# A hybrid encoder block with 32 experts: 0.75 MB of a weight unit loaded by an earlier instruction, and two spread parts placed before the last down product instead of behind it

## The reference, cut to what matters

```python
x = x + jnp.concatenate([a, p], axis=-1) @ w_out[l]
h = rmsnorm(x, xattn_norm_g[l])
x = x + memory_cross_attention(h, rmsnorm(mem, mem_norm_g[l]), ...)   # softmax(q k / sqrt(128)) v @ xo_w
h = rmsnorm(x, ffn_norm_g[l])
x = x + hierarchical_moe(h, ...)
# per expert e, on the tokens routed to it:
(jax.nn.silu(xb @ w_gate[e]) * (xb @ w_up[e])) @ w_down[e]            # 2048 -> 512 -> 2048
```

## Time and profile before

| | us |
|---|---|
| three runs | 1671.82, 1673.2, 1670.22 (median 1671.82) |
| the profiled execution | 1668.66 |
| its span, first to last instruction | 1666.9 |
| PE busy | 1553.7 (93%) |
| DVE busy | 637.7 (38%) |
| ACT busy | 357.5 (21%) |
| data read and written | 484.81 MB and 8.39 MB (millions of bytes) |

### The profile page before, as it was taken

The page is one execution under the profiler, slowest core; times in us unless marked ns, Lnnn a source line. Parts: engine busy times, 40 slices in busy tenths (PEclk is TensorE's granted clock), DMA queues, the critical chain, the costliest instruction groups (busy, mean ns, idle before and its releaser), DMA issues.

```text
span 1666.9 us, 18187 instructions
## 1 busy us (share of the span) xinstructions
PE 1553.7 (93%) x7236; PEld 894.2 (54%) x7236; DVE 637.7 (38%) x774; ACT 357.5 (21%) x639; POOL 165.2 (10%) x235
## 2 busy tenths in 40 slices
PE   7999999999999999799999899889889899899998
PEld 7788777768887567634343433434434334343343
DVE  6656656652223433513233322322323323323224
ACT  6422333352222244211110110011011011101011
POOL 4470044510000000100000000000000000000000
PEclk9999999999999999999999999999999999999999
DMA  8332322353215031799999999999999999999997
GB/s 304 102 101 79 94 61 70 103 183 101 96 56 202 1 127 44 320 377 429 412 424 429 428 428 429 428 423 420 429 417 417 428 420 428 428 426 428 424 421 290
DMA packets 90237, 484.47 MB, mean 291 GB/s; under 512 B 6066, under 2 KB 44108, under 8 KB 62156
## 3 DMA queue, kind: packets, MB, share of 16 engines
q1 hardware_dynamic: 86696, 470.84, 69.8%
q0 software_dynamic: 3392, 12.92, 2.3%
q10 hardware_dynamic: 100, 0.03, 0.0%
HBM read 484.81 MB, written 8.39 MB: 296 GB/s over the span
## 4 chain that ended last, share of the span: by engine, by line
PE 68%; DMA 17%; DVE 8%; ACT 3%; issue 2%; SPq 1%; POOL 0%; DVEq 0%; POOLq 0%; ACTq 0%
PE ps L2232 23%; DMA weight_ring<-in_expert_w_up_dram 15%; PE ps L1939 10%; PE ps L1813 8%; PE ps L2258 8%; PE ps L2193 5%; PE ps L1992 3%; DVE residual L1618 3%; ACT weight_ring L887 1%; PE ps L1775 1%; DMA residual<-in_x_dram 1%; PE ps L2321 1%; PE ps L2056 1%; DVE weight_ring L1290 1%; PE ps L2081 1%
## 5 line engine op out<-in xcount | busy, mean ns | idle before, releaser
L2232 PE MATMUL ps<-weight_ring,transposed_acts 128*64 128x512 f32 x2000 | 467.6, 610 | 40.2 <-DMA weight_ring<-in_expert_w_up_dram 39.4
L2232 PEld LDWEIGHTS ps<-weight_ring,transposed_acts 128*64 128x64 f32 x2000 | 169.0, 140 | 331.6 <-issue 260.1
L1618 DVE TENSOR_TENSOR residual<-ps,residual 128x1024 f32<-128x1024 f32 x128 | 150.8, 1219 | 249.6 <-PE ps L2193 249.2
L2258 PE MATMUL ps<-weight_ring,transposed_acts 128*64 128x512 f32 x960 | 214.1, 599 | 17.8 <-DVE transposed_acts L1628 17.8
L1634 DVE SCALAR_TENSOR_TENSOR y_low<-ps,proj_buffer,y_high 64x1024 fp32r<-64x1024 f32 x60 | 77.0, 1283 | 199.4 <-ACT y_high L1079 198.4
L2258 PEld LDWEIGHTS ps<-weight_ring,transposed_acts 128*64 128x64 f32 x960 | 67.6, 138 | 146.8 <-issue 142.7
L1079 ACT ACTIVATE y_high<-ps,proj_buffer 64x1024 fp32r<-64x1024 f32 x60 | 66.5, 1109 | 288.1 <-PE ps L2258 287.3
L1813 PE MATMUL ps<-mix_high,w_in_high 128*128 128x512 f32 x288 | 117.8, 409 | 1.3 <-issue 1.3
L1068 ACT ACTIVATE transposed_acts<-ps 128x512 f32<-128x512 f32 x32 | 19.1, 598 | 464.7 <-PE ps L2232 464.7
L1813 PE MATMUL ps<-mix_high,w_in_low 128*128 128x512 f32 x288 | 112.8, 392 | 0.0
L1813 PE MATMUL ps<-normed_low,w_in_high 128*128 128x512 f32 x288 | 112.7, 391 | 0.0
(11 more groups left out here) (323 smaller groups left out, 1889.3 us busy)
## 6 DMA issues: line engine op xcount, KB each, us to landing
weight_ring<-in_expert_w_down_dram SPq DMA_DIRECT2D x63, 2048.0 KB, 15.8
weight_ring<-in_expert_w_gate_dram SPq DMA_DIRECT2D x61, 2048.0 KB, 16.3
weight_ring<-in_expert_w_up_dram SPq DMA_DIRECT2D x60, 2048.0 KB, 20.5
weight_ring<-in_w_in_dram SPq DMA_DIRECT2D x18, 1024.0 KB, 5.6
weight_ring<-in_w_out_dram SPq DMA_DIRECT2D x16, 1024.0 KB, 5.0
weight_ring<-in_xkv_w_dram SPq DMA_DIRECT2D x8, 1024.0 KB, 7.6
residual<-in_x_dram SPq DMA_DIRECT2D x8, 1024.0 KB, 12.8
weight_ring<-in_xq_w_dram SPq DMA_DIRECT2D x4, 1024.0 KB, 9.7
```

The source lines that it names most:

```text
L1618: v.tensor_tensor(part, ps[:, bank:bank + 2, :].rearrange("p b n -> p (b n)"), part, ALU.add).then_inc(signal, 1)
L2232: ins = mm(ps[side * SLOTS:(side + 1) * SLOTS, 0, :], xsT[:, k, par * SLOTS:(par + 1) * SLOTS], gate_up_weights(e, u, kk), start=(k == 0), ...
L2258: ins = mm(ps[half, 4 + n % 2, :], act_t[:, f * SLOTS:(f + 1) * SLOTS], w[:, n * 512:(n + 1) * 512], start=(f == 0), stop=(f == KF - 1), s ...
```

## The change

It has two parts.

1. Of expert 1's unit 3 the floats 2048 to 3583 of each partition (the first 1536 floats of slot 7, 0.75 MB) are loaded by an instruction of their own, issued once `oT_ready` has reached 4. What is left, slot 6 (1 MB) and the last 512 floats of slot 7 (0.25 MB), is loaded at the old place by two instructions. The count that PE waits for is raised to match.
2. Of the last pair, parts 2 and 3 are spread by PE and added by DVE before the last half down product and its low part, not behind them.

```diff
                 if u == 0:
+                    sp.wait_ge(oT_ready, NT)
+                    part = slice(CHK, 2 * CHK - 512)
+                    sp.dma_start(unit(3)[:, part], expert_unit(1, 3)[:, part]).then_inc(landed[unit_slot(3)], 16)
                     sp.wait_ge(o_done, 28)
                     sp.wait_ge(parts_done, 32)
-                sp.dma_start(unit(u), expert_unit(1 if u == 3 else 0, u)).then_inc(landed[unit_slot(u)], 16)
+                if u == 3:
+                    for part in (slice(0, CHK), slice(2 * CHK - 512, 2 * CHK)):
+                        sp.dma_start(unit(u)[:, part], expert_unit(1, u)[:, part]).then_inc(landed[unit_slot(u)], 16)
+                    continue
+                sp.dma_start(unit(u), expert_unit(0, u)).then_inc(landed[unit_slot(u)], 16)
@@ DVE, last_blocks
                 last_rest(2)
-                last_part(0)
-                last_part(1)
+                for i in range(4):
+                    last_part(i)
                 last_rest(3)
-                for i in range(2, 2 * NT):
+                for i in range(4, 2 * NT):
                     last_part(i)
@@ PE, expert_landed
                     if u == 3:
-                        loads -= 1
+                        loads += 1
@@ PE, last_blocks
                 pe.wait_ge(y_dve, 2 * NE - 4 + 4)
-                last_part(0)
-                last_part(1)
+                for i in range(4):
+                    last_part(i)
                 last_down_of(3)
-                last_part(2)
-                last_part(3)
                 pe.wait_ge(y_dve, 2 * NE - 4 + 8)
```

## The result

The median of 20 runs is 1672.55 us (1670.38 to 1678.11) against 1669.6 of 20 runs of the kernel before: ratio 1.0019, 95% interval 1.0013 to 1.0024. By the medians the change costs 3.0 us. Its distance of 5.9 to the span before overstates this: it was already 1.6 us late at the first expert load (SP's issue at 609.71 against 608.09), ahead of anything that was changed.

The account below looks back on a forecast made before the run. The prediction took bytes to bound the expert stage from 881, PE close behind. Part 1 at 0 and part 2 at 2.83 - 1.1 = +1.7 us, put on 1671.8, gave 1673.5 us; range 1669.5 to 1677.0.

Parts of the forecast that it names:

- What bounds the kernel, and part 1 at 0: Expert stage bound by bytes from 881; 1.9 us saved at 676 is lost where PE releases loads, so 0.
- The signs: In the profile after: queue near 0 for about 2 us at 715 to 717 and again at 731 to 735.
- A loss is excluded: First gather, issued at 699.22: fewer queued bytes cannot slow it; gain between 0 and 1.9 us, taken as 0.
- The small pieces: Two extra small transfers of part 1: an estimated 4 us by the skill's rule, but no cost expected.
- The new wait: SP's wait for `oT_ready` 4 ends at 642.78, delays nobody; the bytes meet an empty queue; no cost.
- The order of the parts: Tail: parts 2 and 3 first start the last down product 3.86 us later and end the additions 2.83 later.
- The stores: End of the kernel: a row of four instead of six lands its last in 4.2, not 5.3, giving back 1.1.
- The forecast's upper end of 2.8: Part 2's cost at the upper end for the stores: +2.8 us, where +1.7 was forecast.
- The time itself: Whole kernel: 1673.5 us, from a starting median of 1671.8 plus 1.7; this forecast had chance 0.55.
- The lower end of the range: Whole kernel: 1669.5 us, given as the near side of the faster rival.
- The clock rival: Tail: PE's clock falls in the two new gaps; 1676.0 us for both, 1674.3 for only the later; chance 0.20.
- The faster rival: Tail: last weights land late unprofiled, making parts 2 and 3 free; -3.0 with the front paying, or -4; chance 0.08.

Follow-up runs that it names:

- e2_load_only: The changed kernel with the old order of the last parts, so part 1 alone: 1670.43 us against 1670.09 for the kernel before, ratio 1.0002.
- e1_parts_only: The kernel before with only part 2 of the change, parts 2 and 3 before the last down product: 1673.35 us against 1670.09, ratio 1.0024.
- e10_one_store: The kernel before without the stores of parts 0 to 6; one execution, used only for its trace: last store 3.8 us from issue to landing.
- e5_few_busy: The changed kernel with products of constants in PE's two new gaps, 6 before part 2, 9 after the last down product: 1673.99 us against 1670.24, ratio 1.0025.
- e4_small_pieces: The kernel before with part 1 alone, and three 1 MB loads beside the first gather in pieces of 4 KB, not 8 KB: ratio 0.9998.
- e11_smallest_busy: The kernel before with part 1 alone, 2 KB pieces beside the first gather, and 21 products of constants, not 8, ahead of the first transposes: ratio 0.9986.
- e12_down_first: The kernel before with parts 0 and 1 also moved behind the last down product: 1671.36 us against 1670.75, ratio 1.0006.

## Why the prediction was right, and where not

- **What bounds the kernel, and part 1 at 0.** Right, and by the steps given: the queue nearly empty at 716, a pause again at 734 to 736, the gather not sped up (9.12, 9.01), `e2_load_only` at 1.0002. The signs were not quite those named: the queue sagged to 168 GB/s at 718 and 66 at 735 and didn't stand for 2 us at either place, and the stand of a whole microsecond before owed part of its length to the clock (8.57 against 7.09). "A loss is excluded" didn't hold either: the first gather took 8.7 to 9.1 us in the five profiles with the early load beside 8 KB pieces and 8.4 to 8.8 in the four without; what delays it is open. The small pieces cost nothing: by the Trainium skill's "DMA: Bandwidth & Descriptors" they should have, an estimated 4 us (two more transfers at its fixed 2.0 us each), and the trace has 412 GB/s from 699 to 716 as before. The page took its figures with transfers issued from GpSimd; these are issued by SP.
- **The new wait.** SP was to pass it at 642.8; after, it issues at 644.44, 1.6 later as all of the front was. The bytes didn't meet an empty queue, as I had it, but a 1 MB store of POOL's; that cost the store 0.1 us. Nothing in the profile waits for these bytes.
- **The order of the parts.** The start of the last down product was worked out as 3.86 later and is 3.88 in `e1_parts_only`; the last addition as 2.83 and is 2.89.
- **The stores: the term that failed.** They were to give back 1.1, because the fourth store of a row had landed after 4.2. The last one lands after 5.5 and gives nothing back: from the last addition to the end of the span the four kernels with the new tail need 5.6 to 6.0 us, and the eight with the old one 5.7 to 6.1. I took its lateness for a backlog that grows with the row. Between four and eight stores it doesn't grow, and even alone the last store needs 3.8, not 2.7 (`e10_one_store`). With this the sum is 2.9, against 3.0 measured; 1.7 was forecast. The forecast's upper end of 2.8 used the last store's own 5.3, which was the figure to take.
- **The time itself.** That 1673.5 came within 1 us of the measured 1672.55 is partly luck: the three runs that it starts from have a median 2.2 above that of the 20, and the change was put 1.3 too low.
- **Smaller slips.** The rate of 412 GB/s and more starts with slice 19 of the page, at 750 us; slice 18 has 377. The lower end of the range, 1669.5, isn't what its rival comes to (1671.8 - 3.0 = 1668.8).
- **The clock rival.** The clock fell once in the tail of the profiled execution, in the first gap, at a price of 1.5 us. As the cause of the difference to my sum it is refuted by `e5_few_busy`, and by `e1_parts_only`, where it didn't fall either.
- **The faster rival.** The last weights were there in every profile; PE's only waits in the tail are for DVE. Unprofiled executions can't be looked at.

## What to carry to other kernels

In a stage bound by transfers, a byte moved earlier pays only if the queue doesn't run dry before the stage begins; find the last stand of the queue and what releases it, and work on that instead. Putting work ahead of the last link of a chain is free up to the point where that work itself must wait for a shared engine: here two parts were free, and four cost 3 us. The time to landing of the last store must be read from the last store, not from an earlier one of the same row.

## What the hardware showed that I had not expected

- The first gather's time depends on the size of the pieces in the other queue, as long as that queue stays full: it landed after 8.4 to 9.1 us beside 8 KB pieces, 7.4 to 7.8 beside 4 KB, 7.1 beside 2 KB. (In `e10_one_store` it was issued 28 us after the units and not 23, so that the queue ran low while it was served, and landed after 6.6.) The queue's rate hardly paid for it. The packet records show what happens. Between the first and the last of the gather's 144 packets the other queue moves 161 pieces of 8 KB in the kernel before, 163 of 4 KB in `e4_small_pieces` and 184 of 2 KB in `e11_smallest_busy`, in 4.1, 2.7 and 2.0 us: the engines take turns by pieces, about one for one, and not by bytes. "DMA: Bandwidth & Descriptors" in the Trainium skill (section "Queues, rings and completion order") says that each engine goes round between its queues, but that it works off a packet of about 9 to 17 descriptors before it changes. The first half agrees with the trace, the second doesn't.
- One DMA engine of sixteen works for 1 us after the others at the end of `e10_one_store`, behind an instruction fetch of 1.18 us; in `e1_parts_only` two fetches take 2.8 us of engine time in the stretch before.
- PE's clock at the start of block 0 differs between executions of the same code there: 64 products took 14.0 in the kernel before, 16.46 in `e2_load_only`, 16.14 in `e4_small_pieces` and 15.77 in `e12_down_first`.
